# Attention masks moved from TensorE to VectorE and GpSimd, gate selectors in float32r

## The reference

```python
def _stick_breaking_attention(q, k, v):
    mask = kpos[None, :] < tpos[:, None]
    z = einsum(q, k) * scale
    log_1mb = where(mask, log_sigmoid(-z), 0.0)
    between = cumsum(log_1mb, axis=3, reverse=True) - log_1mb
    a = where(mask, exp(log_sigmoid(z) + between), 0.0)
    return einsum(a, v)

def _diff_attention(q1, q2, k1, k2, v, lam):
    mask = kchunk[None, :] <= tchunk[:, None]          # chunks of 64 positions
    p1 = softmax(where(mask, einsum(q1, k1) * scale, NEG_INF))
    p2 = softmax(where(mask, einsum(q2, k2) * scale, NEG_INF))
    return einsum(p1 - lam * p2, v)

def fox_attention(h, w_q, w_o, k, v, c_bhs):
    # scores * scale + c[query] - c[key], c = cumulated log of the forget gate, causal mask, softmax
```

## Time and profile before

| what | value |
|---|---|
| median of 3 runs | 2295.85 us (2295.70 to 2296.21) |
| span of the profiled execution | 2293.8 us |
| TensorE busy | 2270.3 us (99%), 11064 matmuls |
| VectorE busy | 1338.0 us (58%) |
| ScalarE busy | 880.9 us (38%) |
| GpSimd busy | 256.3 us (11%) |
| granted TensorE clock | 9 tenths or more in all 40 slices |
| DMA | 202.79 MB, 88 GB/s over the span |

### The profile page before, as it was taken

One profiled execution on the slowest core, in us unless ns is written; L12 is line 12 of the kernel. 1 busy time (PEld: TensorE's weight loads), 2 busy tenths in 40 slices (PEclk: granted clock), 3 DMA queues, 4 the chain that ended last, 5 costly groups with the idle time before them and its releaser, 6 DMA issues.

```text
span 2293.8 us, 32791 instructions
## 1 busy us (share of the span) xinstructions
PE 2270.3 (99%) x11064; PEld 1840.3 (80%) x11064; DVE 1338.0 (58%) x1913; ACT 880.9 (38%) x1372; POOL 256.3 (11%) x212
## 2 busy tenths in 40 slices
PE   8999999999999999999999999999999999999998
PEld 6777778888888888868888888887777888888887
DVE  5557756543434779965465445486665646454555
ACT  6675645442324521233332222244444333222222
POOL 2022101211010400004040000040000404000003
PEclk9999999999999999999999999999999999999999
DMA  4222223333334333412123333332211222333332
GB/s 144 65 65 62 73 78 98 112 93 101 91 101 124 115 88 116 127 56 74 56 76 99 93 100 101 91 97 66 65 56 56 83 65 80 102 94 92 101 93 91
DMA packets 395616, 202.79 MB, mean 88 GB/s; under 512 B 13792, under 2 KB 393200, under 8 KB 395520
## 3 DMA queue, kind: packets, MB, share of 16 engines
q1 hardware_dynamic: 394672, 199.34, 29.7%
q0 software_dynamic: 848, 2.16, 0.3%
HBM read 198.84 MB, written 2.10 MB: 88 GB/s over the span
## 4 chain that ended last, share of the span: by engine, by line
PE 88%; issue 6%; DVE 2%; ACT 2%; POOL 1%; DMA 1%; DVEq 0%; SPq 0%; ACTq 0%; POOLq 0%
PE bank L1783 24%; PE bank L1785 23%; PE bank L1784 23%; PE bank L2168 2%; PE bank L2160 2%; PE bank L1763 2%; PE bank L2188 1%; PE bank L2266 1%; PE bank L2243 1%; PE bank L2339 1%; PE bank L2375 1%; PE bank L2077 1%; PE bank L2079 1%; PE bank L2078 1%; DVE m_w_lo L1121 1%
## 5 line engine op out<-in xcount | busy, mean ns | idle before, releaser
L608 ACT ACTIVATE m_w_hi<-m_raw 128x1024 fp32r<-128x1024 f32 x332 | 351.5, 1059 | 879.7 <-PE bank L1785 846.7
L1783 PE MATMUL bank<-m_h_hi,m_w_hi 128*128 128x512 f32 x1504 | 608.5, 405 | 2.2 <-DVE m_w_lo L1121 1.2
L1785 PE MATMUL bank<-m_h_hi,m_w_lo 128*128 128x512 f32 x1504 | 587.0, 390 | 0.0
L1784 PE MATMUL bank<-m_h_lo,m_w_hi 128*128 128x512 f32 x1504 | 586.4, 390 | 0.0
L1121 DVE TENSOR_TENSOR m_w_lo<-m_raw,m_w_hi 128x1024 fp32r<-128x1024 f32 x332 | 440.2, 1326 | 92.2 <-ACT m_w_hi L608 87.3
L1783 PEld LDWEIGHTS bank<-m_h_hi,m_w_hi 128*128 128x128 f32 x1504 | 282.8, 188 | 65.9 <-issue 4.7
L1785 PEld LDWEIGHTS bank<-m_h_hi,m_w_lo 128*128 128x128 f32 x1504 | 282.4, 188 | 60.4
L1784 PEld LDWEIGHTS bank<-m_h_lo,m_w_hi 128*128 128x128 f32 x1504 | 283.1, 188 | 55.5 <-issue 2.4
L1783 PE MATMUL bank<-m_f_hi,m_w_hi 128*128 128x512 f32 x688 | 268.7, 391 | 0.2 <-DVE m_w_lo L1121 0.2
L1785 PE MATMUL bank<-m_f_hi,m_w_lo 128*128 128x512 f32 x688 | 267.8, 389 | 0.0
L1784 PE MATMUL bank<-m_f_lo,m_w_hi 128*128 128x512 f32 x688 | 267.7, 389 | 0.0
(11 more groups left out here) (392 smaller groups left out, 3039.6 us busy)
## 6 DMA issues: line engine op xcount, KB each, us to landing
m_raw<-in_ff_w SPq DMA_DIRECT2D x256, 256.0 KB, 3.0
m_raw<-in_conv_pw_w SPq DMA_DIRECT2D x48, 256.0 KB, 4.0
m_raw<-in_w_in SPq DMA_DIRECT2D x47, 256.0 KB, 3.2
m_raw<-in_w_ffn_gate SPq DMA_DIRECT2D x44, 256.0 KB, 3.1
m_raw<-in_w_ffn_up SPq DMA_DIRECT2D x44, 256.0 KB, 3.1
m_raw<-in_w_ffn_down SPq DMA_DIRECT2D x40, 256.0 KB, 2.9
m_raw<-in_w_gate SPq DMA_DIRECT2D x32, 256.0 KB, 3.1
m_mem_w<-in_mem_wk SPq DMA_DIRECT2D x32, 256.0 KB, 3.1
```

Of the source, the lines that this page charges most:

```text
L608: act.activation(WH[:, v % 2], RAW[:, v % 2], ACT.Copy).then_inc(s.w_hi, 1)
L1783: pe.matmul(o, high[:, r, k, :], hi, start=start, stop=False)
L1784: pe.matmul(o, high[:, r, k, :], lo, start=False, stop=False)
L1785: last = pe.matmul(o, low[:, r, k, :], hi, start=False, stop=stop)
```

## The change

1. **Fox and differential attention.** The 64 and 32 mask matmuls are gone. VectorE's reduction, drain and multiplication become one `tensor_tensor_reduce` per map: it adds the mask (now 512 columns wide, zeros before the diagonal block, `NEG_CAUSAL[:, T - w:T]`) to the bank, multiplies by -1 (fox) or -0.125, writes that back to the bank, and keeps its minimum over the row, which is the bias. The exponential reads the bank with scale -1.0. In differential attention each map now signals by itself (8 signals a head instead of 4).
2. **Stick-breaking.** The 32 mask matmuls are gone. GpSimd adds `UNSEEN` to the 8 diagonal blocks of the kept scores of a pair after `sb_masks`, each addition behind the ScalarE copy it needs; VectorE's `exponents` wait for them.
3. **Gates.** `CP` and `SEL` are float32r: two parts instead of three. The selector is loaded in bfloat16 and converted by one ScalarE copy of 128x1024; `forget_parts` on VectorE has fewer passes and waits for that copy; TensorE's own wait for the selector goes.
4. **Small things.** 13 start-up loads instead of 12, the two wide masks being 128 KB each; some tiles at other addresses; VectorE's loops over heads and pairs written out; the lambda semaphores merged into one.

The core of the diff:

```diff
             def sb_unseen(p):
+                for e, t in UNSEEN_ORDER:
+                    d = ZS[e][:, SB_AT[t]:SB_AT[t] + P]
+                    pool.wait_ge(s.sb_kept, p * 6 + ({2: 1, 0: 3, 1: 5}[SB_IN[t][0]] + e))
+                    pool.tensor_tensor(d, d, UNSEEN[:], ALU.add).then_inc(s.sb_unseen, 1)
...
             with pool.Fori(0, PAIRS) as p:
                 sb_masks(p)
+                sb_unseen(p)
...
                 def ex(b):
-                        act.wait_ge(s.da_nm, n * 4 + (b + 1))
                         for c, dst in enumerate((P1, P2)):
-                            act.activation(dst[:, b % 2, 0:w], SBK[(2 * b + c) % 4][:, 0:w], ACT.Exp, scale=0.125,
+                            act.wait_ge(s.da_nm, n * 8 + (2 * b + c + 1))
+                            act.activation(dst[:, b % 2, 0:w], SBK[(2 * b + c) % 4][:, 0:w], ACT.Exp, scale=-1.0,
...
                 step(forget)
+                act.wait_ge(s.sel_in, 16)
+                act.activation(SEL[:], SELB[:], ACT.Copy).then_inc(s.sel_hi, 1)
...
                 def exponents():
                     for e, g, n in BANK_ORDER:
+                        dve.wait_ge(s.sb_unseen, p * 8 + UNSEEN_DONE[e, g])
                         dve.wait_ge(s.sb_c, p * 8 + n)
...
                 def mx(b):
                         for c in range(2):
+                            z = SBK[(2 * b + c) % 4][:, 0:w]
                             dve.wait_ge(s.da_s, n * 8 + (2 * b + c + 1))
-                            dve.reduce_max(ST[:, 8 * b + 4 + c:8 * b + 5 + c], SBK[(2 * b + c) % 4][:, 0:w], AX.X)
-                        dve.drain()
-                        dve.tensor_scalar(ST[:, 8 * b:8 * b + 2], ST[:, 8 * b + 4:8 * b + 6], -0.125, None, ALU.mult)\
-                            .then_inc(s.da_nm, 1)
+                            dve.tensor_tensor_reduce(out=z, in0=z, in1=NEG_CHUNK[:, T - w:T], scale=-0.125,
+                                                     scalar=-LOWEST, op0=ALU.add, op1=ALU.min,
+                                                     accum_out=ST[:, 8 * b + c:8 * b + c + 1]).then_inc(s.da_nm, 1)
...
                     def mx(x):
                             dve.wait_ge(s.fx_s, p * 8 + (x + 1))
-                            dve.reduce_max(ST[:, 16 + x:17 + x], SBK[x % 4][:, 0:w], AX.X)
-                            dve.drain()
-                            dve.tensor_scalar(ST[:, x:x + 1], ST[:, 16 + x:17 + x], -1.0, None, ALU.mult)\
-                                .then_inc(s.fx_nm, 1)
+                            z = SBK[x % 4][:, 0:w]
+                            dve.tensor_tensor_reduce(out=z, in0=z, in1=NEG_CAUSAL[:, T - w:T], scale=-1.0,
+                                                     scalar=-LOWEST, op0=ALU.add, op1=ALU.min,
+                                                     accum_out=ST[:, x:x + 1]).then_inc(s.fx_nm, 1)
...
-                            pe.matmul(block[:, 0:P], IDENTB, UNSEEN[:], start=False, stop=True).then_inc(s.sb_c, 1)
+                            last.then_inc(s.sb_c, 1)
...
                             pe.matmul(SBK[(2 * b + c) % 4][:, 0:w], Q[r:r + 64, b * P:w], K[r:r + 64, 0:w], start=True,
-                                      stop=False)
-                        for c in range(2):
-                            pe.matmul(SBK[(2 * b + c) % 4][:, b * P:w], IDENTB, NEG_CHUNK, start=False, stop=True)\
-                                .then_inc(s.da_s, 1)
+                                      stop=True).then_inc(s.da_s, 1)
...
                                 pe.matmul(banks[e][:, 0:w], SEL[r:r + 64, p, :], CP[r:r + 64, 0:w], start=False,
-                                          stop=False)
-                            for e in range(2):
-                                pe.matmul(banks[e][:, b * P:w], IDENTB, NEG_CAUSAL, start=False, stop=True)\
-                                    .then_inc(s.fx_s, 1)
+                                          stop=True).then_inc(s.fx_s, 1)
```

More of the change, by code:

```diff
@@ L89, in shape_constants @@
         for e in range(2):
-            for part in range(3):
+            for part in range(2):
                 heads[64 * e + 8 * part + p, p, :] = 1.0
@@ L1384, in _ @@
             group(da_evacs(1, (s.da_vt, 1)), *then(da_pieces(0, None), sb_late(PAIRS - 1)))
-            with U.loop(dve, PAIRS - 2, 4) as i:
+            for i in range(PAIRS - 2):
                 group(da_evacs(i + 2, (s.da_vt, i + 2)), *da_pieces(i + 1, i))
```

90 lines of the change are left out of this document (45 added, 45 removed).

## The result

| | before | changed kernel |
|---|---|---|
| median | 2295.89 us (2295.70 to 2296.21, 4 runs) | 2282.47 us (2282.04 to 2283.01, 4 runs) |
| span of the profiled execution | 2293.8 us | 2281.0 us |
| TensorE busy, matmuls | 2270.3 us, 11064 | 2257.7 us, 10936 |
| VectorE / ScalarE / GpSimd busy | 1338.0 / 880.9 / 256.3 us | 1326.6 / 880.2 / 274.0 us |

The account below looks back on a forecast made before the run. TensorE's stream was taken as the bound (2270.3 of 2293.8 us busy). Savings of 7.3 + 1.1 + 2.2 + 1.0 = 11.6 us from 2295.85 gave 2284.2 us, with 2281.5 to 2291.0 for 8 in 10.

Parts of the forecast that it names:

- Fox masks, 7.3: TensorE's fox scores: removing 64 mask matmuls shortens steps by 0.91 us per pair, 7.3 us over 8 pairs.
- rival A: TensorE: most gaps stay as bubbles, or hooked pieces reach their waits early; about 2291 us, chance 0.10.
- Difference masks, 1.1: TensorE in difference attention: removing 32 masks in 16 pieces saves 0.07 us each, 1.1 us.
- Stick-breaking masks, 2.2: TensorE in stick-breaking: removing 32 single masks saves 0.07 us each, 2.2 us, bounds 0 and 4.8.
- Selectors at nothing: TensorE's float32r fox selectors and gates: no time change; at the other end, 2.9 us lost to bare weight loads.
- The new maximum: VectorE's combined instruction at 512 columns: 0.7 us plus 0.1 to 0.2 for the read, 0.05 less than before.
- Rival B: VectorE's new maximum streams at half rate, 1.3 us and the read; 2295 us in all, chance 0.06.
- Rival C: VectorE's new maximum has a large fixed cost, deciding from 0.5 us extra each; about 2310 to 2325, chance 0.05.
- Signals per map, 1.0: Difference attention: the first exponential starts after the first maximum, saving 0.5 us at two places, 1.0, bounds 0 and 1.1.
- GpSimd's additions: Stick-breaking: eight additions per pair, 666 ns each, finish in time; late only over 1.4 us each, delaying value matmuls.
- Slack of 1 us at the transpositions: Fox transpositions on TensorE, except the second: 1 us in hand each before slower VectorE maxima make them wait, an estimate.
- Start-up load: One more start-up DMA: VectorE idles 2.34 us behind these loads, so half a microsecond is hidden, or costs 0.5.

Follow-up runs that it names:

- experiment 1: Changed kernel with the fox part alone undone: 64 mask matmuls back on TensorE, reduction, drain and multiplication on VectorE; 2290.2 us.
- experiment 10: Kernel before, with the 96 mask matmuls of fox and difference attention left out, reductions, drains and multiplications as they were; 2287.85 us.
- experiment 7: Changed kernel with one plain VectorE reduction more before each of the 64 fox maxima; 2283.18 us.
- experiment 9: Changed kernel with gate selectors and cumulated gates in bfloat16 and three parts again; 2282.70 us.
- experiment 12: Changed kernel with difference attention undone (mask matmuls, reductions, one signal for both maps) and VectorE's loop over the middle heads a loop again; 2285.11 us.
- experiment 6: Changed kernel with each GpSimd addition of the stick-breaking mask made three times, with drains between; 2295.75 us.
- experiment 8: Changed kernel with two plain VectorE reductions more before each fox maximum; 2297.07 us.
- experiments 3: Changed kernel with the stick-breaking part alone undone: 32 mask matmuls on TensorE, no GpSimd additions; 2285.7 us.
- experiment 5: Changed kernel with GpSimd's squares of the first difference head put back before the additions of the last stick-breaking pair; 2282.46 us.

## Why the prediction was right, point by point

- **Fox masks, 7.3.** Measured 7.2 by starts, 7.7 by experiment 1. Reading the price as "steps that remain" from neighbours without a mask was right to 0.04 at both places, and experiment 10 shows that in seven pairs it is all TensorE's. That the sum fits so well is in part luck: by themselves the masks gave 6.9, because in the last pair TensorE came to its wait too early, which the prediction has only as rival A; there the shorter maxima, put at nothing, brought the other 0.4 (that they are what did it is argued from what one reduction more costs at this place, 0.72 in experiment 7).
- **Difference masks, 1.1.** Measured 1.3: a pair of masks was 0.08 before a unit's product, not 0.07. Without the new maxima and signals only 0.7 of it was to be had (experiment 10).
- **Stick-breaking masks, 2.2.** Measured 2.4, 0.076 for each, from the neighbour's step of 0.12, which is 0.11 now. The gap behind a short float32r matmul was not filled but was there anyway, as assumed.
- **Selectors at nothing.** Held to about 0.3 us (experiment 9); the other end, 2.9 were the longer load bare once per piece, did not come.
- **The new maximum.** Forecast 0.7 and a bare read; it took 0.71, and the read runs beside the next instruction. Rival B's half rate would have been 1.3 and is out; so is C's large fixed cost: 579 and 713 ns at 384 and 512 columns leave a fixed part of about 0.18, near that of the other forms.
- **Signals per map, 1.0.** The step of the prediction that was mis-sized, with its bound of 1.1 passed: 1.7. Two things were missed. The idle time of 0.56 in the earlier trace rows is not what a gap costs, which was 0.73 by starts and 0.1 more in the matmuls behind it; and the written-out loop, put at "only change instruction fetches", takes 0.2 off the same chain (experiment 12). The signal by itself was worth 0.47 a gap, so the 0.5 taken for it was right, and the shorter maxima, put at nothing here too, brought 0.16.
- **GpSimd's additions.** They took 585 ns in the records and 0.52 to 0.58 from one to the next, eight in 4.12 us in the last pair; VectorE never waited. The limit of 1.4 each lies between the 1.5 and 1.25 of experiment 6, but what is late beyond it are the next pair's scores and the first squares, not the value matmuls.
- **Slack of 1 us at the transpositions.** Too small: two reductions of up to 0.69 before each pair of maxima cost nothing in six of eight pairs (experiment 7). Rival C's point of decision at 0.5 extra was therefore too early; between 0.55 to 0.69 and twice that is where it lies (experiment 8).
- **Not foreseen:** 0.45 because GpSimd's squares moved behind its new additions and no longer slow VectorE's subtraction (experiments 3 and 5), and 0.3 at two unit starts of the first head, open in part.
- **Start-up load.** Hidden, as said: VectorE's small products wait 1.52 us for the last load, and 1.73 us of idle are still behind them, where there were 2.34:

```profile
24.57 0.35 DVE L1204 TENSOR_TENSOR m_lams<-m_lams 1x64 f32<-1x64 f32 x2 [1.52 <-DMA m_neg_causal<-in_narrow]
...
27.06 0.88 DVE L1234 TENSOR_SCALAR m_rs_diagonals<-m_con,m_stats 128x128 f32<-128x128 f32 x4 [1.73 <-ACT m_stats L712]
```


## What to carry to other kernels

Where one engine is 99% busy, price an instruction by the distance between starts around it and around a neighbour without it, not by its duration, and a wait by the start-to-start gap less the stream's own step, not by the idle time that a view shows. When work moves to an idle engine, ask what it pushes back in that engine's queue and what it will then run beside: here it made one operation of another engine 0.65 us shorter, and repeating the additions made TensorE wait for the next pair of heads, not for the one they belong to. A slack that is only assumed is best loaded with extra work: of this prediction's two, the one at the transpositions was far too small, and the other had its size but not the place where it runs out. And what a removed instruction saves alone can be less than what it saves beside a faster feeding engine: here 7.7 us for fox and difference masks alone, some 8.5 with the rest.

## What the hardware showed that was not expected

- VectorE's subtraction of 128x1024 took 1.88 us while GpSimd multiplied tiles of 128x512 and 1.23 us while it didn't (experiment 5); beside GpSimd's work it also took 2.04 at 224.08 (experiment 12). In both places it ends 1.08 us after the GpSimd instruction that was running when it started (159.07 to 160.15, 225.04 to 226.12), and the GpSimd product behind that one, started at 225.00, took 2.24. The rows look as if the two took turns instruction by instruction, although the program ties neither to the other; that was not tested further.
- The accumulator read of the new maximum (142 ns) starts together with the next instruction of VectorE (229.07 twice), so it costs nothing in a row of maxima.
- A loop on VectorE in place of the written-out code shows idle times marked issue of 0.2 us and made TensorE's step at each of two places 0.2 longer (experiment 12). Pauses of 0.43 to 0.47 marked issue also come singly, at other places from kernel to kernel (experiments 3, 9 and 12), and TensorE then stood 0.33 and 0.36 at fox's second transposition in experiments 3 and 9.
